# Moving one weight sum and the last adds of a Strassen-like MLP to GpSimd and ScalarE, and two sines to a later place

## The chip, the cores and the metric

The kernel runs on one core of one Trainium2 chip. The metric is the device time of one execution in microseconds (us), from its first to its last instruction with the small constant around them; lower is better.

## The reference, cut to what matters

Two transformer blocks run one after the other on x, 512 tokens by 1024 features, all in float32. The change lies in the MLP at the end of the first block, and at its border to the second block:

```python
# first_block, last two lines
h2 = rms_norm(x, norm_mlp_g[l])
x = x + jnp.square(jax.nn.relu(h2 @ w_up[l])) @ w_down[l]      # 1024 -> 4096 -> 1024
# second_block, first lines
cos_m, sin_m = rope_angles(positions, MLA_ROPE_DIM)            # sines and cosines of 28 angles a token
h = rms_norm_2(x, norm_gain[l])
proj = h @ w_in[l]
```

## The kernel before, in words

Every large product is made of three matmuls in a reduced float32 format: both operands are split into a high part (a rounded copy) and a low part (the rest), and high times high, high times low and low times high are summed in PSUM. ScalarE makes the high part of the weights (`split_hi`, `weight_hi`, tile `w_hi`), VectorE the low part by a subtraction (`split_lo`, `weight_lo`, tile `w_lo`); the same goes for the operands (`operand_hi`, `operand_lo`, tiles `op_hi` and `op_lo`). The order on each engine is written out by hand, and the engines are tied by counting semaphores.

The MLP is cut into 4 chunks of 1024 hidden features (`chunk(c)` on ScalarE and on VectorE, `mlp_up` and `mlp_down` on TensorE). In a chunk, TensorE first makes 8 tiles of the up projection, 24 matmuls of 512 columns each (L313), in the two banks of `proj` by turns; ScalarE takes each through a Relu and a Square into `acts` (L751, L753). Then comes the down projection of the chunk, in which the 2 by 2 blocks of `acts` and of the weights are combined by a scheme with 7 products in place of 8 (L1834). Three of the seven products are kept in PSUM over all four chunks (`RES`, six banks of `pa` and `pm`; the function `product` counts them in `res_made`) and are added to the residual stream `x_res` only at the end, by `drain` on VectorE (L1299 to L1309). The other four go through `proj` and are added to `x_res` in each chunk (tiles 8 to 15 of the chunk, `add`, L1321). TensorE waits with the next use of a bank of `proj` until the add before it has freed it (`tile_free`), and with each product until its weights and operands are there (`d_lo` counts the weights, `a_lo` the operands).

The combinations need sums of weight blocks. `t_two` is one of them; `w_sum[:, 0, 4:8]`, which is `t_two` less block `b21`, is another, of 128 x 2048 values. It shares its memory with a part of `w_lo` that the up projection reads until the chunk's eighth tile is done. `angles` (arguments of the sines) and `drained` share memory with `t_two`.

In the last chunk the third RMS norm and the first tiles of the second block follow without a pause: `norm_rstd(2, t)` on ScalarE, `token_scale(2, t)` on VectorE (L373), `token_turn(2, t)` on TensorE (8 transposes, L381), `token_hi` and `token_lo`. The last of the seven products is split for them: half of it (L1868, 12 matmuls), the transposes of token block 0, the other half, the transposes of block 1.

At the start of the MLP the first two tiles of the up projection are made in halves of 256 columns. The third tile needs the bank of the first, which ScalarE frees with its Relu.

Of the kernel before, what the change touches and what calls it, by code (L numbers as in the profile page):

```python
# [9 lines left out]
ALU = mybir.AluOpType  # L10
# [3 lines left out]
P = 128  # L14
# [68 lines left out]
def program(nc, x_in, wall, gains, head_par, sb_gains, b_if, *rest):  # L83
    *block2_in, out = rest
    with ExitStack() as ctx:
# [79 lines left out]
        b11, b21 = w_raw[:, 0], w_raw[:, 1]  # L165
        (a11, a12), (a21, a22) = [[acts[:, 4 * j:4 * j + 4, 2 * P * i:2 * P * (i + 1)] for j in range(2)] for i in range(2)]
# [90 lines left out]
        RES = (pa[:, 0:512], pa[:, 512:1024], pa[:, 1024:1536], pm[:, 0:512], pm[:, 512:1024], pm[:, 1024:1536])  # L257
# [218 lines left out]
        def _(pool):  # L476
# [52 lines left out]
            for r in (1, 2):  # L529
                if r == 2:  # L530
                    gp.wait_ge(S["t_made"], 4 * CHUNKS)
                gp.dma_start(row_gain[r][:, :], norm_rows[r - 1:r].broadcast_to([P, DM])).then_inc(S["rows_landed"], 16)
# [4 lines left out]
            gp.memset(causal[:, :], 0.0).then_inc(S["causal0"], 1)  # L537
            gp.wait_ge(S["causal0"], 1)
# [28 lines left out]
        def _(act):  # L567
# [165 lines left out]
            a.wait_ge(S["angles"], len(ANGLES))  # L733
            a.activation(sine[:, :, :], A3, ACT.Sin)
            a.activation(cosine[:, :, :], C3, ACT.Sin).then_inc(S["trig"], 1)
            a.preload_act_table_set("natural_log_exp_and_others")

# [6 lines left out]
            def chunk(c):  # L744
# [34 lines left out]
                operand_hi(0, a21)  # L779
                a.wait_ge(S["res_made"], 3 * c + 2)  # L780
# [11 lines left out]
            with a.Fori(0, CHUNKS) as c:  # L792
                chunk(c)

# [259 lines left out]
        def _(dve):  # L1054
# [236 lines left out]
            def drain(c, u):  # L1291
                x = [x_res[:, 2 * i + u, 512 * j:512 * (j + 1)] for i in range(2) for j in range(2)]
                z = drained[:, u]
                if u == 0:
                    v.wait_ge(S["res_made"], 3 * CHUNKS)
                    v.wait_ge(S["t_made"], 4 * CHUNKS)
                    v.wait_ge(S["d_lo"], 7 * c + 6)
                v.wait_ge(S["tile_free"], T_MLP + 16 * c + 9 + 4 * u)
# [9 lines left out]
                for i in (2, 3):  # L1308
                    v.tensor_tensor(x[i], x[i], z, ALU.add).then_inc(S["r_sum"], 1)  # L1309
                v.wait_ge(S["r_sum"], 7 * u + 7)  # L1310

            def chunk(c, first=False, last=False):
# [52 lines left out]
                if last:  # L1365
                    drain(c, 0)
# [803 lines left out]
```

## Time and profile before

| | |
|---|---|
| median of 3 runs | 1238.46 us (1238.39 to 1240.06) |
| the profiled execution, its own time | 1240.14 us |
| its span, first to last instruction | 1237.9 us |
| TensorE busy | 1217.6 us, 98% of the span |
| VectorE busy | 784.2 us, 63% |
| ScalarE busy | 637.1 us, 51% |
| GpSimd busy | 72.1 us, 6% |

A busy time is the share in which an instruction is in flight. TensorE's 20.3 us without one lie in few places, so these places, and not the shares, say what there is to be had. The profiled execution is 1.7 us above the median of the runs.

### The profile page before, as it was taken

What the parts mean: (1) busy time and instruction counts of PE and PEld (TensorE: products, weight loads), DVE (VectorE), ACT (ScalarE), POOL (GpSimd) and SP (SyncE); (2) the same over time, 40 slices, a digit from 0 to 9 for tenths busy, and PEclk for the clock granted to TensorE, in tenths of its full rate; (3) what the DMA queues carried; (4) which work ended last, traced back from release to release, by engine and by line L of the source; (5) the groups of instructions that cost most, each with busy time, mean ns of one, the idle gap of its engine ahead of it and who ended that gap; (6) DMA issues with size and microseconds to landing.
All of it is one profiled execution on the core that took longest, in us unless ns stands there. A gap on an engine that the chain in (4) does not pass through costs nothing.

```text
span 1237.9 us, 15568 instructions
## 1 busy us (share of the span) xinstructions
PE 1217.6 (98%) x5820; PEld 991.9 (80%) x5820; DVE 784.2 (63%) x1226; ACT 637.1 (51%) x926; POOL 72.1 (6%) x148
## 2 busy tenths in 40 slices
PE   8999999999999999999999999989999999999998
PEld 7888888888888888888888888868867777777887
DVE  7735544683564466469377483797579989656671
ACT  7635544563564462554444452545466555566820
POOL 2101110210111021000000000000000000000000
PEclk9999999999999999999999999999999999999999
DMA  5321322322132226214216123124213333535621
GB/s 212 123 95 39 110 68 76 102 88 95 37 111 68 77 102 224 102 34 148 91 40 216 50 102 136 34 85 162 77 68 111 113 135 111 218 123 179 238 69 68
DMA packets 25605, 134.21 MB, mean 108 GB/s; under 512 B 3336, under 2 KB 3512, under 8 KB 12752
## 3 DMA queue, kind: packets, MB, share of 16 engines
q1 hardware_dynamic: 16224, 107.14, 25.1%
q0 software_dynamic: 4720, 16.90, 3.9%
q10 hardware_dynamic: 4608, 9.44, 2.0%
q8 instruction: 35, 0.57, 0.2%
q14 instruction: 18, 0.15, 0.0%
HBM read 121.92 MB, written 11.55 MB: 108 GB/s over the span
## 4 chain that ended last, share of the span: by engine, by line
PE 87%; DVE 9%; issue 2%; ACT 1%; DMA 0%; ACTq 0%; DVEq 0%
PE proj L313 64%; PE proj L1834 5%; PE pm L1834 2%; PE pa L1834 2%; PE pm L1748 1%; PE pa L1759 1%; PE pa L2024 1%; DVE w_lo L286 1%; PE pa L1720 1%; PE pm L1730 1%; DVE idx L1468 1%; PE proj L1769 1%; PE pa L1769 1%; PE pa L2004 1%; PE pa L1739 1%
## 5 line engine op out<-in xcount | busy, mean ns | idle before, releaser
L313 PE MATMUL proj<-h_hi,w_hi 128*128 128x512 f32 (+1 forms) x848 | 332.5, 392 | 3.6 <-ACT acts L751 2.6
L313 PE MATMUL proj<-h_hi,w_lo 128*128 128x512 f32 (+1 forms) x848 | 327.7, 386 | 0.0
L313 PE MATMUL proj<-h_lo,w_hi 128*128 128x512 f32 (+1 forms) x848 | 327.3, 386 | 0.0
L286 DVE TENSOR_TENSOR w_lo<-w_raw,w_hi 128x2048 fp32r<-128x2048 f32 x84 | 191.5, 2288 | 58.7 <-ACT w_hi L280 58.4
L280 ACT ACTIVATE w_hi<-w_raw 128x2048 fp32r<-128x2048 f32 x84 | 159.6, 1913 | 67.3 <-PE proj L1834 46.9
L313 PEld LDWEIGHTS proj<-h_hi,w_hi 128*128 128x128 f32 x848 | 159.8, 188 | 39.8 <-issue 6.4
L313 PEld LDWEIGHTS proj<-h_hi,w_lo 128*128 128x128 f32 x848 | 159.6, 188 | 32.5
L313 PEld LDWEIGHTS proj<-h_lo,w_hi 128*128 128x128 f32 x848 | 159.8, 188 | 31.9 <-issue 1.0
L313 PE MATMUL proj<-w_hi,h_hi 128*128 128x512 f32 (+1 forms) x288 | 112.8, 392 | 0.3 <-issue 0.3
L313 PE MATMUL proj<-w_lo,h_hi 128*128 128x512 f32 (+1 forms) x288 | 111.6, 388 | 0.0
L313 PE MATMUL proj<-w_hi,h_lo 128*128 128x512 f32 (+1 forms) x288 | 111.4, 387 | 0.0
L751 ACT ACTIVATE acts<-proj 128x512 f32<-128x512 f32 x32 | 19.0, 594 | 97.8 <-PE proj L313 97.8
L313 PEld LDWEIGHTS proj<-w_hi,h_hi 128*128 128x128 f32 x288 | 54.1, 188 | 14.1 <-issue 3.5
L313 PEld LDWEIGHTS proj<-w_lo,h_hi 128*128 128x128 f32 x288 | 54.0, 188 | 10.9
L313 PEld LDWEIGHTS proj<-w_hi,h_lo 128*128 128x128 f32 x288 | 54.1, 188 | 10.4
L945 ACT ACTIVATE p_sb<-p_sb,mx 128x128 f32<-128x128 f32 (+1 forms) x64 | 35.2, 551 | 28.6 <-DVE mx L1557 28.6
L1834 PE MATMUL proj<-w_hi,op_hi 128*128 128x512 f32 x120 | 46.9, 391 | 2.5 <-DVE x_res L1321 2.5
L1834 PE MATMUL proj<-w_hi,op_lo 128*128 128x512 f32 x120 | 46.7, 389 | 0.0
L1834 PE MATMUL proj<-w_lo,op_hi 128*128 128x512 f32 x120 | 46.7, 389 | 0.0
L1329 DVE TENSOR_TENSOR w_sum<-b,b 128x2048 f32<-128x2048 f32 x4 | 9.2, 2292 | 56.8 <-PE proj L313 56.8
L1166 DVE SCALAR_TENSOR_TENSOR tok<-pm,floor 128x4 f32<-128x4 f32 x8 | 1.3, 162 | 67.9 <-ACT y_tok L659 67.9
L1321 DVE TENSOR_TENSOR x_res<-x_res,proj 128x512 f32<-128x512 f32 x40 | 26.7, 683 | 12.7 <-PE proj L1834 12.1
(455 smaller groups left out, 2083.7 us busy)
## 6 DMA issues: line engine op xcount, KB each, us to landing
w_raw<-in_wall SPq DMA_DIRECT2D x92, 1024.0 KB, 5.0
b<-in_wall SPq DMA_DIRECT2D x8, 1024.0 KB, 6.1
gates<-gate_st ACTq DMA_DIRECT2D x24, 256.0 KB, 2.0
m_all<-gates POOLq DMA_DIRECT2D x2, 1280.0 KB, 7.8
x_res<-in_x ACTq DMA_DIRECT2D x4, 512.0 KB, 5.1
bc<-gate_rows POOLq DMA_DIRECT2D x8, 256.0 KB, 3.4
x_res<-in_x POOLq DMA_DIRECT2D x4, 512.0 KB, 4.2
x<-x_res POOLq DMA_DIRECT2D x1, 2048.0 KB, 7.7
```

What stands on the lines that cost most here:

```text
L280: nc.scalar.activation(w_hi[:, slot, 4 * half:4 * half + 4, :], w_raw[:, half], ACT.Copy)\
L286: nc.vector.tensor_tensor(w_lo[:, slot, 4 * half:4 * half + 4, :], w_raw[:, half], w_hi[:, slot, 4 * half:4 * half + 4, :], ALU.subtract)\
L313: mm = nc.tensor.matmul(proj[:, bank, 0:cols] if tokens else proj[:, bank, toks], lhsT, rhs, start=(k == 0 and q == 0), stop=(k == kts - 1 ...
L751: a.activation(acts[:, i], proj[:, i % 2], ACT.Relu).then_inc(S["tile_free"], 1)
L945: a.activation(x, x, ACT.Exp, bias=mx[:, u, i:i + 1], accum_out=row_sum[:, u, i:i + 1])\
L1321: done = v.tensor_tensor(x, x, proj[:, i % 2], op)
L1468: v.scalar_tensor_tensor(idx[:, c], rel[h % 2][:, c], w_idx[:, i, h:h + 1], idx[:, c] if h else causal[:, 384 - P * i:512], ALU.mult, ALU. ...
L1720: mm = t_.matmul(pa[:, LOW[i]:LOW[i] + P * (i + 1)], a_[:, 0, P * i:P * (i + 1)], b_[:, 1, 0:P * (i + 1)], start=(x == 0), stop=(x == 2))
L1730: mm = t_.matmul(pm[:, TRI[i]:TRI[i] + SEQ - P * i], keys[r, P * i:P * (i + 1)], queries_[r, P * i:], start=True, stop=True)
L1739: mm = t_.transpose(pa[:, o:o + P], beta[:, LOW[i] + P * j:LOW[i] + P * (j + 1)], ident[:, :])
L1769: mm = t_.matmul(out_bank(t), y[:, k, c], w[:, 1, k, :], start=(k == 0 and q == 0), stop=(k == KT - 1 and q == 2))
L1834: mm = t_.matmul(banks[u], x[:, operand, k, P * u:P * (u + 1)], w[:, slot, 4 * half + k, :], start=(start and k == 0 and q == 0), stop=(st ...
```

## The change

Four edits, all in the MLP and at its end:

- The sum `w_sum[:, 0, 4:8]` is made by GpSimd in each of the 4 chunks, in place of VectorE. It starts when the first kept product of the chunk is made (`res_made`).
- The sines and cosines are computed by ScalarE behind the second Relu and Square of the first chunk, in place of ahead of the first weight copies of the chunk.
- The kept products are drained in another way: ScalarE copies the first two banks to `drained`, VectorE adds the other four, GpSimd adds the partial sums to `x_res`, in eight additions of 128 x 512. Two banks of `RES` change places for it.
- In the last chunk VectorE's order is another.

```diff
-        RES = (pa[:, 0:512], pa[:, 512:1024], pa[:, 1024:1536], pm[:, 0:512], pm[:, 512:1024], pm[:, 1024:1536])
+        RES = (pa[:, 0:512], pa[:, 512:1024], pa[:, 1024:1536], pm[:, 1024:1536], pm[:, 0:512], pm[:, 512:1024])
...
+            for c in range(CHUNKS):
+                gp.wait_ge(S["t_made"], 4 * c + 3)
+                gp.wait_ge(S["b21_landed"], 16 * c + 16)
+                gp.wait_ge(S["res_made"], 3 * c + 1)
+                gp.tensor_tensor(w_sum[:, 0, 4:8], t_two[:, :, :], b21, ALU.subtract).then_inc(S["t_made"], 1)
+            gp.wait_ge(S["d_lo"], 7 * CHUNKS - 4)
...
+            for u in range(2):
+                gp.wait_ge(S["r_sum"], u + 1)
+                gp.tensor_tensor(x_quarter[u][0][0], x_quarter[u][0][0], drained[:, u], ALU.add).then_inc(S["x_drained"], 1)
+            for u in range(2):
+                gp.wait_ge(S["r_sum"], u + 3)
+                gp.tensor_tensor(x_quarter[u][0][1], x_quarter[u][0][1], drained[:, u], ALU.add).then_inc(S["x_drained"], 1)
+            gp.wait_ge(S["tile_free"], T_END1 - 4)
+            for u in range(2):
+                gp.wait_ge(S["r_sum"], u + 5)
+                for j in range(2):
+                    gp.tensor_tensor(x_quarter[u][1][j], x_quarter[u][1][j], drained[:, u], ALU.add).then_inc(S["x_drained"], 1)
...
-            a.wait_ge(S["angles"], len(ANGLES))
-            a.activation(sine[:, :, :], A3, ACT.Sin)
-            a.activation(cosine[:, :, :], C3, ACT.Sin).then_inc(S["trig"], 1)
-            a.preload_act_table_set("natural_log_exp_and_others")
...
                 for i in range(4):
                     square(i)
+                    if first and i == 1:
+                        a.wait_ge(S["angles"], len(ANGLES))
+                        a.activation(sine[:, :, :], A3, ACT.Sin)
+                        a.activation(cosine[:, :, :], C3, ACT.Sin).then_inc(S["trig"], 1)
+                        a.preload_act_table_set("natural_log_exp_and_others")
...
+                if last:
+                    a.wait_ge(S["t_made"], 4 * c + 4)
+                    a.wait_ge(S["d_lo"], 7 * c + 3)
+                    for u in range(2):
+                        a.activation(drained[:, u], RES[u], ACT.Copy).then_inc(S["r_sum"], 1)
...
+            def drain_add(u, r, after):
+                v.wait_ge(S["x_drained"], after)
+                v.tensor_tensor(drained[:, u], drained[:, u], RES[r + u], ALU.add).then_inc(S["r_sum"], 1)
...
                 operand_lo(0, a21, c, 5)
-                v.tensor_tensor(w_sum[:, 0, 4:8], t_two[:, :, :], b21, ALU.subtract).then_inc(S["t_made"], 1)
                 weight_lo(1, 1, b12[:, :, :], c, 5)
```

What this makes of three places of the program. On GpSimd, between the load of the first norm's gains and the store of `x_res` to memory (`x`), there stood before:

```order
L532 DMA row_gain_84<-in_norm_rows 128x1024
L532 DMA row_gain_85<-in_norm_rows 128x1024 [waits t_made]
L535 DMA x<-x_res 128x4x1024 [waits tile_free]
```

and now:

```order
L530 DMA row_gain_84<-in_norm_rows 128x1024
L535 TENSOR_TENSOR w_sum<-t_two,w_raw 128x2048 [waits res_made,b21_landed,t_made] x4
L538 DMA row_gain_85<-in_norm_rows 128x1024 [waits t_made,d_lo]
L541 TENSOR_TENSOR x_res<-x_res,drained 128x512 [waits r_sum] x2
L544 TENSOR_TENSOR x_res<-x_res,drained 128x512 [waits r_sum] x2
L549 TENSOR_TENSOR x_res<-x_res,drained 128x512 [waits r_sum,tile_free]
L549 TENSOR_TENSOR x_res<-x_res,drained 128x512
L549 TENSOR_TENSOR x_res<-x_res,drained 128x512 [waits r_sum]
L549 TENSOR_TENSOR x_res<-x_res,drained 128x512
L552 DMA x<-x_res 128x4x1024 [waits tile_free]
```

GpSimd has 12 new instructions with two inputs from SBUF each; the load of the second gains stands behind four of them. On VectorE in the last chunk, around the first half of the drain (`b_82` is the block `b22`; `w_lo`, `op_lo` are the low parts of weights and operands, and `x_res<-x_res,proj` are the adds of tiles 8 and 9), the rows were:

```order
L1285 TENSOR_TENSOR w_lo<-b_82,w_hi 128x2048 [waits d_hi]
L1321 TENSOR_TENSOR x_res<-x_res,proj 128x512 [waits tile_made,tile_free]
L1299 TENSOR_TENSOR x_res<-x_res,pa 128x512 [waits d_lo,tile_free,t_made,res_made]
L1300 COPY drained<-pa 128x512
L1302 TENSOR_TENSOR drained<-drained,pm 128x512 [waits r_sum]
L1304 TENSOR_TENSOR x_res<-x_res,drained 128x512 [waits r_sum]
L1306 TENSOR_TENSOR drained<-drained,pa 128x512 [waits r_sum]
L1309 TENSOR_TENSOR x_res<-x_res,drained 128x512 [waits r_sum]
L1309 TENSOR_TENSOR x_res<-x_res,drained 128x512
L1321 TENSOR_TENSOR x_res<-x_res,proj 128x512 [waits tile_made,tile_free,r_sum]
```

and now:

```order
L1317 TENSOR_TENSOR drained<-drained,pm 128x512 [waits x_drained,res_made]
L1317 TENSOR_TENSOR drained<-drained,pm 128x512 [waits x_drained]
L1309 TENSOR_TENSOR w_lo<-b_82,w_hi 128x2048 [waits d_hi]
L1328 TENSOR_TENSOR x_res<-x_res,proj 128x512 [waits tile_made,tile_free,x_drained]
L1313 TENSOR_TENSOR op_lo<-acts,op_hi 128x1024 [waits a_hi]
L1328 TENSOR_TENSOR x_res<-x_res,proj 128x512 [waits tile_made,tile_free]
L1328 TENSOR_TENSOR x_res<-x_res,proj 128x512 [waits tile_made,tile_free,x_drained]
L1328 TENSOR_TENSOR x_res<-x_res,proj 128x512
L1317 TENSOR_TENSOR drained<-drained,pa 128x512 [waits x_drained]
L1317 TENSOR_TENSOR drained<-drained,pm 128x512 [waits x_drained]
```

Seven instructions between the adds of tiles 8 and 9 are gone, as are seven between tiles 12 and 13; four remain, and three of VectorE's steps now wait for GpSimd (`x_drained`). On ScalarE, where the MLP begins (behind the last `token_hi` of the second norm), there stood:

```order
L734 ACT_TABLE_LOAD
L734 ACTIVATE sine<-angles_100 128x112 [waits angles]
L735 ACTIVATE cosine<-angles_102 128x112
L736 ACT_TABLE_LOAD
L280 ACTIVATE w_hi<-w_raw 128x2048 [waits tile_made]
L280 ACTIVATE w_hi<-w_raw 128x2048 [waits tile_made,w_landed1]
L751 ACTIVATE acts<-proj 128x512 [waits tile_free,tile_made]
```

and now:

```order
L281 ACTIVATE w_hi<-w_raw 128x2048 [waits tile_made,w_landed0]
L281 ACTIVATE w_hi<-w_raw 128x2048 [waits tile_made,w_landed1]
L763 ACTIVATE acts<-proj 128x512 [waits tile_free,tile_made]
L765 ACTIVATE acts<-acts 128x512 [waits tile_free]
L763 ACTIVATE acts<-proj 128x512 [waits tile_made]
L765 ACTIVATE acts<-acts 128x512 [waits tile_free]
L773 ACT_TABLE_LOAD
L773 ACTIVATE sine<-angles_100 128x112 [waits angles]
L774 ACTIVATE cosine<-angles_102 128x112
L775 ACT_TABLE_LOAD
```

The two sines and their two table loads have moved behind the first two Relus.

## Rows read from the trace of the kernel before

**Rows 1.** The page: busy time, share of the span, instructions of each engine.

```profile
PE 1217.6 (98%) x5820; PEld 991.9 (80%) x5820; DVE 784.2 (63%) x1226; ACT 637.1 (51%) x926; POOL 72.1 (6%) x148
```

**Rows 2.** Stretches: length, busy time by engine (instructions), granted clock, DMA share, GB/s.

```profile
552.00:796.00 244.00, 244.00 (x1078) 202.03 (x1077) 157.47 (x108) 110.39 (x101) 0.00 (x0) 1.00 0.30 104
796.00:835.00 39.00, 36.20 (x157) 28.77 (x155) 37.02 (x34) 22.22 (x19) 0.53 (x1) 1.00 0.19 64
```

**Rows 3.** TensorE's waits from 490 to 860: total, times, longest.

```profile
PE pa L381 <- DVE xs L373: 3.6, 1, 3.6
PE proj L313 <- ACT acts L751: 2.6, 1, 2.6
PE proj L1834 <- DVE x_res L1321: 2.5, 1, 2.5
```

**Rows 4.** TensorE in order of time: start, length, instruction, idle before.

```profile
513.81 0.28 PE L313 MATMUL proj<-h_hi,w_lo 128*128 128x256 f32 x1
...
806.79 0.39 PE L1834 MATMUL pm<-w_hi,op_hi 128*128 128x512 f32 x1
...
823.07 0.50 PE L1834 MATMUL proj<-w_hi,op_hi 128*128 128x512 f32 x1 [2.49 <-DVE x_res L1321]
...
834.31 0.39 PE L1868 MATMUL proj<-w_lo,op_hi 128*128 128x512 f32 x1
838.34 1.70 PE L381 MATMUL pa<-ident,xs 128*128 128x128 f32 x8 [3.65 <-DVE xs L373]
839.69 0.78 PE L1868 MATMUL proj<-w_hi,op_hi 128*128 128x512 f32 x1
...
843.66 1.03 PE L381 MATMUL pm<-ident,xs 128*128 128x128 f32 x8
```

**Rows 5.** The chain that ended last: start, length, what, how many.

```profile
516.69 34.55 PE proj L313 x144
...
752.55 43.53 PE proj L313 x192
```

**Rows 6.** ScalarE in order of time, where the MLP begins.

```profile
506.54 1.28 ACT L734 ACT_TABLE_LOAD   x1
...
512.44 3.71 ACT L280 ACTIVATE w_hi<-w_raw 128x2048 fp32r<-128x2048 f32 x2
516.06 0.58 ACT L751 ACTIVATE acts<-proj 128x512 f32<-128x512 f32 x1
```

**Rows 7.** VectorE in order of time, in the last chunk.

```profile
801.13 1.23 DVE L1353 TENSOR_TENSOR acts<-acts,op_sum 128x1024 f32<-128x1024 f32 x1
802.27 2.28 DVE L1285 TENSOR_TENSOR w_lo<-t_two,w_hi 128x2048 fp32r<-128x2048 f32 x1
804.47 1.22 DVE L1289 TENSOR_TENSOR op_lo<-op_sum,op_hi 128x1024 fp32r<-128x1024 f32 x1
...
817.50 0.69 DVE L1299 TENSOR_TENSOR x_res<-x_res,pa 128x512 f32<-128x512 f32 x1
...
837.01 1.28 DVE L373 SCALAR_TENSOR_TENSOR xs<-x_res,rstd,row_gain 128x1024 f32<-128x1024 f32 x1
```

**Rows 8.** GpSimd in order of time: two selects.

```profile
50.72 0.29 POOL L510 TENSOR_SCALAR_AFFINE_SELECT keep<-keep 128x128 f32<-128x128 f32 x1
...
127.76 2.37 POOL L515 TENSOR_SCALAR_AFFINE_SELECT decay<-decay 128x128 f32<-128x128 f32 x1
```

**Rows 9.** GpSimd's groups by shape: busy us, mean ns.

```profile
L539 POOL TENSOR_SCALAR_AFFINE_SELECT causal<-causal 128x128 f32<-128x128 f32 x1 | 0.3, 287 | 0.1
...
L488 POOL CAST wg_lo<-wg_zero 128x704 fp32r<-128x704 f32 x1 | 0.8, 778 | 0.0
```

**Rows 10.** VectorE, one subtraction in order of time.

```profile
127.68 2.29 DVE L286 TENSOR_TENSOR w_lo<-w_raw,w_hi 128x2048 fp32r<-128x2048 f32 x1 [0.24 <-ACT w_hi L280]
```

**Rows 11.** VectorE's lines of one tile: ns min/median/max, first and last start.

```profile
L1138 DVE TENSOR_TENSOR silu<-silu,conv x8: 784/789/790, 50.8 to 440.6; 128x512 f32<-128x512 f32 x8
...
L1185 DVE TENSOR_TENSOR silu<-silu,gate_a x8: 691/693/695, 80.9 to 463.3; 128x512 f32<-128x512 f32 x8
```

More of the change, by code:

```diff
@@ L165, in program @@
         b11, b21 = w_raw[:, 0], w_raw[:, 1]
+        x_quarter = [[[x_res[:, 2 * i + u, 512 * j:512 * (j + 1)] for j in range(2)] for i in range(2)] for u in range(2)]
         (a11, a12), (a21, a22) = [[acts[:, 4 * j:4 * j + 4, 2 * P * i:2 * P * (i + 1)] for j in range(2)] for i in range(2)]
@@ L536, in _ @@
             gp.wait_ge(S["norm_turned"], KT + 2 * TB)
-            gp.memset(causal[:, :], 0.0).then_inc(S["causal0"], 1)
-            gp.wait_ge(S["causal0"], 1)
+            gp.memset(causal[:, :], 0.0).then_inc(S["c0"], 1)
+            gp.wait_ge(S["c0"], 3)
             gp.affine_select(out=causal[:, 384:512], in_=causal[:, 384:512], compare_op=ALU.is_ge, fill=NEG,
@@ L742, in operand_hi, with chunk @@
                 a.activation(op_hi[:, slot], src, ACT.Copy).then_inc(S["a_hi"], 1)
-            def chunk(c):
+            def chunk(c, first=False, last=False):
                 g = G_MLP + 2 * c
@@ L790, in chunk @@
                 split_hi(g + 2, 1, 1, used=n + 12)
-            with a.Fori(0, CHUNKS) as c:
+            chunk(0, first=True)
+            with a.Fori(1, CHUNKS - 1) as c:
                 chunk(c)
+            chunk(CHUNKS - 1, last=True)
             a.preload_act_table_set("natural_log_exp_and_others")
@@ L1359, in chunk @@
                 operand_lo(0, a21, c, 5)
-                v.tensor_tensor(w_sum[:, 0, 4:8], t_two[:, :, :], b21, ALU.subtract).then_inc(S["t_made"], 1)
                 weight_lo(1, 1, b12[:, :, :], c, 5)
                 operand_lo(1, a12, c, 6)
+                if last:
+                    v.wait_ge(S["res_made"], 3 * c + 3)
+                    for u in range(2):
+                        drain_add(u, 4, u + 1)
                 weight_lo(0, 0, b22[:, :, :], c, 6)
+                if last:
+                    v.wait_ge(S["x_drained"], 2)
                 add(8, 0, j=0)
+                operand_lo(2, a22, c, 7)
+                add(9, 1, j=0)
                 if last:
-                    drain(c, 0)
-                add(9, 1, j=0)
-                operand_lo(2, a22, c, 7)
+                    v.wait_ge(S["x_drained"], 4)
                 add(10, 0, 2, j=1)
+                if last:
+                    for u in range(2):
+                        drain_add(u, 2, u + 3)
+                    add(11, 1, 3, j=1)
                 v.wait_ge(S["t_made"], 4 * c + 4)
                 weight_lo(0, 1, w_sum[:, 0, 4:8], c, 7)
-                add(11, 1, 3, j=1)
-                split_lo(g + 2, 1, 0)
+                if not last:
+                    add(11, 1, 3, j=1)
+                    split_lo(g + 2, 1, 0)
                 add(12, 0, j=1)
-                if last:
-                    drain(c, 1)
-                else:
+                if not last:
                     split_lo(g + 2, 1, 1)
@@ L1380, in chunk @@
                 if last:
+                    split_lo(g + 2, 1, 0)
                     token_scale(2, 0)
                     split_lo(g + 2, 1, 1)
+                    v.wait_ge(S["x_drained"], 8)
                 add(14, 2, j=0, op=ALU.subtract)
```

27 lines of the change are left out of this document (3 added, 24 removed).

## The prediction

> **What bounds the kernel now.** I read the page's totals first: TensorE has a matmul in flight for 1217.6 of 1237.9 us [rows 1]. Only its 20.3 us of idle time, and slow stretches, can be won, and anything that makes it wait is lost in full. Next the table of stretches: from 552 to 796, three of the four chunks, TensorE is busy for all of the 244 us, VectorE for 157 [rows 2]. Nothing can be won there; a new wait can only cost. In 796 to 835, the down projection of the last chunk, VectorE is busy for 37.0 of 39 us and TensorE misses 2.8 [rows 2]: here VectorE is the bound. The list of TensorE's waits then names the three places that the edits touch: 2.6 us for a Relu of ScalarE at the start of the MLP, 2.5 us for an add and 3.6 us for a norm scaling of VectorE at its end [rows 3].
>
> **The sines.** TensorE stops at 513.9 and goes on at 516.69, when ScalarE has freed the first bank [rows 3, 4, 5]. ScalarE reached this Relu at 516.06, behind two weight copies of 3.71 us together, which began at 512.44 though the norm's last copy ended at 506.5 [rows 6]. Without table loads and sines ahead of them the copies end near 510.3, and the Relu only has to wait for its tile, which the chip makes before 513.9. The 2.8 us go. The 144 matmuls behind the wait took 34.55 us, where 192 at full rate took 43.53 [rows 5], which is 32.65 for 144: another 1.9 us went to a stretch at the lower of the two clock levels, which I take to follow the idle time. So this edit is worth -4.7 us. In their new place the sines and two table loads take about 3.2 us (they end at 512.44 at the latest, and 2 x 1.28 of it is loads [rows 6]) between the second and the third Relu, 5.4 us apart (24 matmuls of 0.227 us, from 43.53/192 [rows 5]): hidden.
>
> **The weight sum on GpSimd.** VectorE loses a subtraction of 2.2 us a chunk, behind which, in chunks 0 to 2, nobody waits. What GpSimd's version costs is seen in no row; it has two inputs in SBUF and 2048 columns. Its cast of 704 columns took 0.78 us with one input [rows 9]: 2048 columns are 2.25 us for one pass, 4.5 us if the two inputs are read one after the other. These are the bounds of its length T. I take 4.5, since the rows below show the two engines to take turns at reading. By the Trainium skill ("GPSIMD Engine Reference", Performance versus the Vector engine) such a subtraction of 2048 takes 4497 ns; the sum would be the same.
>
> The question is what it does to VectorE. A select of GpSimd takes 0.29 us alone [rows 9]. One that began at 127.76, just behind a VectorE subtraction with two SBUF inputs (127.68, 2.29 us [rows 10]), took 2.37 us [rows 8] and ended 0.15 us after it: it was shut out for the whole instruction. The other way round, the product of 512 columns that VectorE begins at 50.76 in each head, 0.04 us behind a select of 0.29 us (50.72 [rows 8]), takes 0.79 us, the same shape elsewhere 0.69 [rows 11]: it waits until the select's short read is over. GpSimd also gets its turn between VectorE instructions that stand back to back. So I expect that VectorE's instructions with two SBUF inputs wait for GpSimd's whole T. The Trainium skill says so too ("SBUF — State Buffer", Who interferes with whom: the shared pair is an exclusive lock, and the second to issue fully blocks); this trace agrees, for short instructions.
>
> Where it falls: GpSimd may start when the first kept product is done, 5.44 us (24 x 0.227) into the down projection; in the last chunk, whose third product begins at 806.79 [rows 4], that is 5.44 us earlier, 801.35. VectorE is in a combination of `acts` until 802.3, then come the low part of `t_two` (802.27) and of operand 2 (804.47, done at 805.6) [rows 7]. TensorE wants both for the third kept product at 806.79 [rows 4]. The slack is 1.2 us. If GpSimd takes its turn at 802.3, the third product starts T - 1.2 late: 3.3 us with T = 4.5, 1.05 with 2.25. This is the same in each chunk. For chunks 0 to 2: +9.9 us (+3.1 at the lower bound). ScalarE's copies behind it are not held up, and the load that waits for the sum (`t_made`) now starts within 2 us of its old time, with 5 us to spare.
>
> **The last chunk and the norm.** I carry the chain through with the durations of rows 7: 2.2 us a weight part, 1.14 an operand part, 0.6 to 0.7 an add of 512, 1.2 the norm scaling; a GpSimd add of 512 columns is a quarter of T, 1.2 us. The drain of 817.50 and its twin (seven instructions, some 5 us each) no longer stand ahead of the adds for which TensorE waited at 823.07 and ahead of the scaling at 837.01 [rows 4, 7].
>
> If GpSimd did not disturb VectorE: the 2.5 us wait goes, small waits of 0.6 us go, the fifth to seventh products run without a gap until 831.3, the scaling of block 0 is ready at 832.7 in place of 838.3, and everything behind is 5.6 us earlier. The 1.8 us of lower clock behind the wait of 3.65 us go too (transposes 838.34 to 839.69 in place of 0.79 us, half product 839.69 to 843.66 in place of 2.72 [rows 4]). Together -7.4 us.
>
> If it does: the third product ends at 815.5, the fourth at 821.0. VectorE has the low parts at 809.1 and 810.2, then takes turns with GpSimd's first two adds (1.2 us each), has the last operand before the drain at 819.3, two drain adds at 820.7, waits for GpSimd's third add until 821.1, makes the low part of `b22` until 823.3 and frees tile 8 at 823.9. TensorE waited for it since 821.0: +3.0 us. The seventh product's first half ends at 837.6. The scaling of block 0 waits for GpSimd's adds of the second half, which alternate with two weight parts of VectorE, and is done at 841.1, where it was 838.3. So +2.9 us for the last chunk as a whole, with its gains and losses; its old lower clock stays.
>
> **The clock.** Of the three waits of 2.5 to 3.65 us, two had a stretch at the lower level behind them, at 1.9 and 1.8 us. In the locked case there are five new waits of 3.0 to 3.3 us. I take two of them to cost 1.8 us each: +3.6; the bounds are none and five (0 and +9).
>
> **The sum**, against the profiled execution's own 1240.14 us: -4.7 +9.9 +2.9 +3.6 = +11.7, 1251.8; against the median of the runs, which is 1.7 lower, about 1250.2 us.
>
> **The rivals.**
> - No lock that matters: GpSimd's long read is served in between, or it gets its turn only once VectorE pauses (one late turn, after the part of operand 2, would hold up nothing, since the weight part after it ends at 804.47 + 1.14 + 2.2 = 807.8 and is wanted at 806.79 + 5.44 = 812.2). For it: all seen cases are reads of 128 to 256 columns. Against it: a select was shut out for 2.3 us, and got its turn at once when the subtraction ended. Then -4.7 - 7.4 = -12.1: 1226.4 us.
> - A short T. It decides the sign: the loss of the first three chunks is 3(T - 1.2), and below T of about 3 us it no longer eats the gains. At 2.25: -4.7 +3.1 -3.2 -1.8 = -6.6: 1231.9 us.
> - The end of the MLP gives back what it wins, through waits of three engines for each other (`r_sum`, `x_drained`), and GpSimd costs nothing else: the sines alone remain, -4.7: 1233.8 us.
> - The wait at 513.9 stays, because the halves of 256 columns cause the lower clock and not the idle time: this would add 1.9 us to each of the cases.
>
> **Chances.** Locked for a T of 3.5 us or more, 0.61: 1243 (T of 4, no lower clock) to 1256 (T of 4.5, all five). No lock that matters 0.25; short T 0.07; sines alone 0.07. The first is the forecast, its own range 1243 to 1256. Within 0.2% (2.5 us, about what a measurement of this kernel tells from no change) falls only a T near 3 us: 0.03, out of the first and third. The range that leaves out no more than 2 in 10 reaches down into the case without a lock: 1226 to 1256.
>
> **What the profile of the changed kernel would show.** GpSimd's four subtractions: length 5 us or more, of which the first 0.9 is the wait; VectorE's low part of `t_two` at 6.5 us in place of 2.29; TensorE idle for 3.3 us ahead of the third kept product in all four chunks, released by VectorE's operand part; a chunk 85 us long in place of 81.6. Without a lock VectorE's row stays at 2.29 and the chunk at 81.6. TensorE without an idle time near 514 and no matmul of 0.43 us there would show the sines' part right. The scaling of block 0 tells the end of the chunk. Most likely to make me wrong is how GpSimd reads two inputs of 2048 columns: no row shows it.

## The result, and the profile after

The changed kernel takes 1252.14 us (median of 6 runs, 1249.11 to 1253.78), the kernel before 1239.18 us (6 runs, 1238.39 to 1240.06): a ratio of 1.0102, 95% interval 1.0093 to 1.0112. The forecast was 1250.2 us, slower. The profiled execution took 1250.44 us, with a span of 1248.7.

The page of the changed kernel, its totals (the answer to [rows 1]):

```profile
PE 1217.8 (98%) x5820; PEld 991.0 (79%) x5820; DVE 791.4 (63%) x1212; ACT 638.3 (51%) x928; POOL 111.2 (9%) x160
```

TensorE has the same work in the same 1217.8 us. All that was lost is idle time. The table of stretches says where, with columns as in [rows 2]:

```profile
552.00:796.00 244.00, 234.22 (x1018) 192.66 (x1017) 157.31 (x101) 104.78 (x95) 15.46 (x3) 0.99 0.29 101
796.00:835.00 39.00, 33.26 (x146) 26.93 (x145) 31.24 (x18) 19.56 (x17) 15.00 (x6) 1.00 0.16 57
634.00:719.00 85.00, 81.77 (x355) 67.27 (x354) 54.70 (x35) 36.41 (x33) 5.16 (x1) 0.98 0.28 99
```

In 552 to 796 TensorE now misses 9.8 of 244 us, where it missed none. From one third kept product to the next (560.77, 647.45 and 733.98 below and in the table) a chunk lasts 86.7 and 86.5 us, where it lasted 81.6; in 634 to 719, a length of 85, TensorE works for 81.8. TensorE's waits (the answer to [rows 3]):

```profile
PE pm L1851 <- DVE op_lo L1313: 13.1, 4, 3.3
PE pa L382 <- DVE xs L374: 3.5, 1, 3.5
PE proj L1851 <- DVE x_res L1328: 2.4, 1, 2.4
```

Four waits of 3.3 us for VectorE's low part of an operand are new. The wait of 2.6 us for a Relu is gone. The wait for the scaling is about as long as it was, and so is the one for an add of VectorE, but that is now the add of tile 8 and no longer that of tile 9. The reason for the four, in the last chunk, GpSimd first:

```profile
810.63 5.16 POOL L535 TENSOR_TENSOR w_sum<-t_two,w_raw 128x2048 f32<-128x2048 f32 x1 [79.99 <-PE pa L1851]
...
829.86 3.33 POOL L544 TENSOR_TENSOR x_res<-x_res,drained 128x512 f32<-128x512 f32 x1
```

Then VectorE (the answer to [rows 7]):

```profile
810.07 1.23 DVE L1360 TENSOR_TENSOR acts<-acts,op_sum 128x1024 f32<-128x1024 f32 x1
811.22 6.72 DVE L1309 TENSOR_TENSOR w_lo<-t_two,w_hi 128x2048 fp32r<-128x2048 f32 x1
817.86 1.21 DVE L1313 TENSOR_TENSOR op_lo<-op_sum,op_hi 128x1024 fp32r<-128x1024 f32 x1
818.99 3.37 DVE L1309 TENSOR_TENSOR w_lo<-w_raw,w_hi 128x2048 fp32r<-128x2048 f32 x1
822.28 2.31 DVE L1313 TENSOR_TENSOR op_lo<-acts,op_hi 128x1024 fp32r<-128x1024 f32 x1
...
831.98 0.68 DVE L1328 TENSOR_TENSOR x_res<-x_res,proj 128x512 f32<-128x512 f32 x1
832.57 1.70 DVE L1313 TENSOR_TENSOR op_lo<-acts,op_hi 128x1024 fp32r<-128x1024 f32 x1
...
847.83 2.28 DVE L374 SCALAR_TENSOR_TENSOR xs<-x_res,rstd,row_gain 128x1024 f32<-128x1024 f32 x1
```

GpSimd starts at 810.63, waits until VectorE's combination ends at 811.30, and is done at 815.79: 4.49 us of its own. VectorE's low part of `t_two`, 2.28 us long before, lasts from 811.22 to 817.94: its own 2.2 us begin when GpSimd has ended. Where VectorE has one input in PSUM, GpSimd's reading costs it nothing: the add of a tile of `proj` at 831.98 takes its usual 0.68 us inside GpSimd's add (829.86 to 833.19). The operand part behind it, both inputs in SBUF, waits for GpSimd's end and takes 1.70 in place of 1.22. Even the norm scaling (847.83) is held up. TensorE in order of time (the answer to [rows 4]):

```profile
560.77 0.47 PE L1851 MATMUL pm<-w_hi,op_hi 128*128 128x512 f32 x1 [3.32 <-DVE op_lo L1313]
...
562.26 0.63 PE L1851 MATMUL pm<-w_lo,op_hi 128*128 128x512 f32 x1
...
815.51 0.39 PE L1851 MATMUL pm<-w_lo,op_hi 128*128 128x512 f32 x1
819.21 0.47 PE L1851 MATMUL pm<-w_hi,op_hi 128*128 128x512 f32 x1 [3.32 <-DVE op_lo L1313]
...
832.80 0.47 PE L1851 MATMUL proj<-w_hi,op_hi 128*128 128x512 f32 x1 [2.42 <-DVE x_res L1328]
...
850.16 0.33 PE L382 MATMUL pa<-ident,xs 128*128 128x128 f32 x1 [3.50 <-DVE xs L374]
```

A matmul of 0.39 us is one at the full rate, of 0.63 one at the lower of the two clock levels; they start 0.23 and 0.43 us apart. Both kernels run the same 5820 matmuls in the same order, so that the start of one can be set against the start of the same one. The column on the right is the sum of all gains and losses up to there:

| matmul, by its number in the trace | before | after | after less before |
|---|---|---|---|
| 2484, behind the Relu | 516.69 | 513.74 | -2.95 |
| 2496, behind the lower clock of before | 521.05 | 516.49 | -4.56 |
| 2676, third kept product, chunk 0 | 561.96 | 560.77 | -1.19 |
| 2688, behind a lower clock | 564.68 | 565.18 | +0.50 |
| 3036, third kept product, chunk 1 | 643.59 | 647.45 | +3.86 |
| 3043, behind a lower clock | 645.17 | 650.53 | +5.36 |
| 3396, third kept product, chunk 2 | 725.19 | 733.98 | +8.79 |
| 3410, behind that wait | 728.36 | 737.31 | +8.94 |
| 3756, third kept product, chunk 3 | 806.79 | 819.21 | +12.43 |
| 3816, behind the add of tile 9 | 823.07 | 835.62 | +12.55 |
| 3864, transposes of block 0 | 838.34 | 850.16 | +11.82 |
| 3877, in the last half product | 841.97 | 852.25 | +10.28 |
| 3972, second block | 860.10 | 870.93 | +10.82 |

ScalarE where the MLP begins (the answer to [rows 6]):

```profile
506.22 3.71 ACT L281 ACTIVATE w_hi<-w_raw 128x2048 fp32r<-128x2048 f32 x2
511.06 0.60 ACT L763 ACTIVATE acts<-proj 128x512 f32<-128x512 f32 x1 [1.13 <-PE proj L314]
...
515.22 1.28 ACT L773 ACT_TABLE_LOAD   x1
```

The copies begin 6.2 us earlier, and the Relu waits for its tile, not for ScalarE.

### The profile page after: what moved, and what is told of

Same layout as the page of the kernel before. It is cut to its first block, busy times and chain, and to the rows that moved or that the text cites. A ratio compares the mean times of both kernels' runs of the same rounds, so it can differ in the third digit from the quotient of the medians.

```text
span 1248.7 us, 15534 instructions
## 1 busy us (share of the span) xinstructions
PE 1217.8 (98%) x5820; PEld 991.0 (79%) x5820; DVE 791.4 (63%) x1212; ACT 638.3 (51%) x928; POOL 111.2 (9%) x160
## 4 chain that ended last, share of the span: by engine, by line
PE 88%; DVE 8%; issue 2%; ACT 1%; DMA 0%; ACTq 0%; DVEq 0%
PE proj L314 64%; PE proj L1851 6%; PE pm L1851 2%; PE pa L1851 2%; DVE w_lo L287 2%; PE pm L1765 1%; PE pa L1776 1%; PE pa L2041 1%; PE pa L1737 1%; PE pm L1747 1%; DVE idx L1485 1%; PE proj L1786 1%; PE pa L1786 1%; DVE op_lo L1313 1%; PE pa L2021 1%
## 5 line engine op out<-in xcount | busy, mean ns | idle before, releaser
L535 POOL TENSOR_TENSOR w_sum<-t_two,w_raw 128x2048 f32<-128x2048 f32 x4 | 20.6, 5156 | 324.2 <-PE pa L1851 324.2
```

The costliest lines, as they stand in the source:

```text
L535: gp.tensor_tensor(w_sum[:, 0, 4:8], t_two[:, :, :], b21, ALU.subtract).then_inc(S["t_made"], 1)
```

## The experiments

Each time stands beside runs of the kernel before on the same chip (1239.3 to 1239.9 us); the ratio is to these. Of each trace I show what decides. "Interval" is the 95% one.

### The weight sum back on VectorE

```diff
-            for c in range(CHUNKS):
-                ...
-                gp.tensor_tensor(w_sum[:, 0, 4:8], t_two[:, :, :], b21, ALU.subtract).then_inc(S["t_made"], 1)
...
                 operand_lo(0, a21, c, 5)
+                v.tensor_tensor(w_sum[:, 0, 4:8], t_two[:, :, :], b21, ALU.subtract).then_inc(S["t_made"], 1)
```

> The changed kernel with one thing undone: the weight sum of every chunk is made by VectorE again, behind operand_lo(0, a21). The sines' new place, the new drain and VectorE's other order stay. Theory (GpSimd's long subtraction shuts VectorE out; this, and not the drain, is the loss): the three waits of 3.3 us in chunks 0 to 2 go and the two stretches at the lower clock behind them, 5.06 + 4.86 + 3.55 = 13.5 us by the shift of TensorE's matmuls between the two traces. In the last chunk ScalarE's copies to drained now wait for VectorE's sum and stand ahead of the high part of b12, so that TensorE waits about 5.3 us for tile 8 in place of 3.3 and 2.7 us: that chunk stays within 1 us of the changed kernel's. About 1237 us, VectorE's low part of t_two at 2.28 us, chunks 81.6 us apart. Rival (the drain with GpSimd is what costs, through waits of three engines for each other): no less than 1245 us.

1240.02 us, ratio 1.0001 (interval 0.9991 to 1.0010). The waits:

```profile
PE proj L1847 <- DVE x_res L1323: 5.2, 1, 5.2
PE pa L382 <- DVE xs L374: 3.5, 1, 3.5
```

The four waits are gone; 12.1 us come back, so that GpSimd's sum is the loss. The absolute time was expected 3 us lower. The wait for tile 8 came as expected (5.2), but 10 matmuls ran at the lower clock behind it (2.1 us), and from chunk 2 to the second block this kernel loses 5.1 us against the one before (-4.5 to +0.6 by the matmuls), the changed one 1.9 (+8.9 to +10.8): 3.2 more, not within the 1 us allowed.

### The sines alone, and the sum alone

The kernel before with ScalarE's edit alone:

```diff
-            a.activation(sine[:, :, :], A3, ACT.Sin)
...
+                    if first and i == 1:
+                        ...
+                        a.activation(sine[:, :, :], A3, ACT.Sin)
```

> The kernel before with the sines' move alone. Theory: -4.7 us as forecast (the traces of the two kernels show -4.4 us by TensorE's shift there): about 1234.7 us against 1239.2; no idle time near 514, ScalarE's third Relu waits for its tile. Rival (what is won at the start of the MLP is given back at its end, where VectorE is the bound and its work hangs on loads and not on TensorE): within 1 us of the kernel before.

1235.34 us, ratio 0.9967 (0.9954 to 0.9979), 4.5 us less. TensorE's matmuls are 4.64 us earlier at the first kept products and 4.66 us earlier at the transposes of block 0: nothing is given back. And the kernel before with GpSimd's sum alone:

```diff
+                    for c in range(CHUNKS):
+                        ...
+                        gp.wait_ge(S["res_made"], 3 * c + 1)
+                        gp.tensor_tensor(w_sum[:, 0, 4:8], t_two[:, :, :], b21, ALU.subtract).then_inc(S["t_made"], 1)
...
-                v.tensor_tensor(w_sum[:, 0, 4:8], t_two[:, :, :], b21, ALU.subtract).then_inc(S["t_made"], 1)
```

> The kernel before with the weight sum on GpSimd alone, started behind the first kept product of each chunk as in the change; sines and drain as before. Theory: 3.4 us in each of chunks 0 to 2, 2.3 us in the last one (VectorE has 2.28 us less to do there, so that the wait of 2.5 us shrinks to 1.5), which is 12.5 us, and up to two or three stretches at the lower clock of 1.5 to 1.7 us each: 1252 to 1256 us against 1239.2. Rival (the loss comes only with the sines' move or the new drain): 1243 us or less.

1259.37 us, ratio 1.0163 (1.0146 to 1.0180), above the range. The waits are those expected:

```profile
PE pm L1840 <- DVE op_lo L1295: 13.1, 4, 3.3
PE pa L381 <- DVE xs L373: 2.8, 1, 2.8
PE proj L313 <- ACT acts L757: 2.6, 1, 2.6
PE proj L1840 <- DVE x_res L1327: 2.4, 1, 2.4
```

What was mis-sized is the lower clock. It followed the waits of chunks 0, 1 and 3 and that for tile 9, for 13, 7, 13 and 9 matmuls: 42 x 0.20 = 8.4 us where at most 5 had been allowed. The wait for tile 9 did not shrink to 1.5. This trace also lacks the two lower-clock stretches of the kernel before, behind the Relu wait and behind the scaling (by the shift of the matmuls -1.6 us each), though both waits are there: whether a stretch follows a wait is not settled by the wait alone.

### The sum in pieces, and half of it

```diff
-                gp.tensor_tensor(w_sum[:, 0, 4:8], t_two[:, :, :], b21, ALU.subtract).then_inc(S["t_made"], 1)
+                for k in range(4):
+                    piece = gp.tensor_tensor(w_sum[:, 0, 4 + k], t_two[:, k], b21[:, k], ALU.subtract)
+                piece.then_inc(S["t_made"], 1)
```

> The changed kernel with GpSimd's weight sum in four instructions of 512 columns in place of one of 2048, at the same place; the work and the bytes are the same. GpSimd's adds of 512 columns took 1.3 us in the changed kernel. Theory (an instruction of one engine with two SBUF inputs holds out that of the other until it has ended, and the engines take turns between instructions): VectorE's part of t_two waits for one piece and takes about 3.4 us in place of 6.7, the operand part behind it waits for the next one and takes 2.3, so that TensorE waits for 2 x 1.15 less the slack of 1.2, about 1.2 us in place of 3.3, in each of the four chunks: 2.1 us less in each, and less or nothing of the 3.2 us at the lower clock: 1240.5 to 1244 us. Rival (the two engines share the memory's rate, so that the same bytes in the same stretch cost the same): the wait stays at 3.3 us and the time at 1250 to 1252.

1248.07 us, ratio 1.0065 (1.0048 to 1.0082). VectorE in chunk 0:

```profile
552.94 3.39 DVE L1311 TENSOR_TENSOR w_lo<-t_two,w_hi 128x2048 fp32r<-128x2048 f32 x1
556.25 2.30 DVE L1315 TENSOR_TENSOR op_lo<-op_sum,op_hi 128x1024 fp32r<-128x1024 f32 x1
558.48 3.38 DVE L1311 TENSOR_TENSOR w_lo<-w_raw,w_hi 128x2048 fp32r<-128x2048 f32 x1
```

And TensorE's waits:

```profile
PE proj L1853 <- DVE x_res L1330: 6.5, 4, 5.0
PE pm L1853 <- DVE op_lo L1315: 4.2, 4, 1.1
```

The same bytes at the same place cost 1.1 us a chunk in place of 3.3, with exactly the lengths that turn-taking gives (3.4 and 2.3). A shared rate is out. The time was missed: the pieces went on to hold up VectorE four times over (3.39, 2.30, 3.38 and 2.31 us), so that TensorE waited 0.5 us for the add of tile 8 in each of chunks 0 to 2, and in the last one the high part of b12 stood behind the late sum, with 5.0 us of wait for tile 8.

```diff
-                gp.tensor_tensor(w_sum[:, 0, 4:8], t_two[:, :, :], b21, ALU.subtract).then_inc(S["t_made"], 1)
+                gp.tensor_tensor(w_sum[:, 0, 4:6], t_two[:, 0:2], b21[:, 0:2], ALU.subtract).then_inc(S["c0"], 1)
...
                 operand_lo(0, a21, c, 5)
+                v.wait_ge(S["c0"], c + 3)
+                v.tensor_tensor(w_sum[:, 0, 6:8], t_two[:, 2:4], b21[:, 2:4], ALU.subtract).then_inc(S["t_made"], 1)
```

> The changed kernel with GpSimd's weight sum at its place, but of half the columns (1024); VectorE makes the other half behind operand_lo(0, a21), in 1.2 us. Theory (what TensorE waits is GpSimd's length less a slack of 1.2 us): GpSimd needs 2.3 us in place of 4.5, VectorE's part of t_two takes 4.5 us in place of 6.7, and TensorE waits about 1.1 to 1.3 us ahead of the third kept product in place of 3.3. In the last chunk ScalarE's copies wait for VectorE's half with b12 behind them, as in the first experiment (1240.0 us). 1240.0 + 3 x 1.2 = 1243.6, up to 1246 with the lower clock. Rival (a fixed price of a switch between the engines, not the length): 3 us a chunk remain, 1248 us or more.

1244.79 us, ratio 1.0038 (1.0023 to 1.0052), inside the range. VectorE, then TensorE's waits:

```profile
552.88 4.51 DVE L1309 TENSOR_TENSOR w_lo<-t_two,w_hi 128x2048 fp32r<-128x2048 f32 x1
```

```profile
PE pm L1853 <- DVE op_lo L1313: 4.3, 4, 1.1
```

GpSimd's half took 2.94 us, 0.65 of it the wait for VectorE's combination. The wait follows the length: 3.3 us for 4.5, 1.1 for 2.3, none without it. So each us of GpSimd's read beyond the slack of 1.2 is a us of TensorE's. In the last chunk the wait for tile 8 was 5.0 us, as in the first experiment.

### The sum on GpSimd, but later

Four kernels, each the changed one with the sum of chunks 0 to 2 at a place where VectorE should have room. First behind the low part of `b22`:

```diff
                 gp.wait_ge(S["res_made"], 3 * c + 1)
+                if c < CHUNKS - 1:
+                    gp.wait_ge(S["d_lo"], 7 * c + 6)
```

> The changed kernel, with GpSimd's weight sum of chunks 0 to 2 started later: behind VectorE's sixth low part of weights (b22), in place of behind the first kept product. It is as long and reads the same; the last chunk is untouched. Theory (the loss is the lock, at a place where VectorE has only 1.2 us of slack): at the new place VectorE's add of tile 8 reads PSUM and its part of operand a22 has over 3 us of slack, so that the 3.3 us waits in chunks 0 to 2 go and nothing or up to 0.5 us a chunk comes in their place (the add of tile 11 stands behind the low part of w_sum). 1250.4 - 13.5 = about 1237 us, up to 1239. Which VectorE instruction is long moves: the part of t_two is 2.28 us again, that of operand a22 about 5 us in place of 1.2. Rival (a sum on GpSimd costs its 3.4 us a chunk wherever it stands, for instance through the load that waits for it, which starts 10 us later): 1248 us or more.

1250.41 us, ratio 1.0091 (1.0073 to 1.0109): the rival's number, not mine. VectorE in chunk 0:

```profile
567.77 5.33 DVE L1315 TENSOR_TENSOR op_lo<-acts,op_hi 128x1024 fp32r<-128x1024 f32 x1
573.02 1.99 DVE L1330 TENSOR_TENSOR x_res<-x_res,proj 128x512 f32<-128x512 f32 x3
```

The operand part is the long one, as expected, and it had the room. What I had not followed is the queue: the add of tile 9 stands behind it, at 573.02, and TensorE wanted its bank at 571.0. Waits of 2.6 us took the place of those of 3.3 in three chunks (the fourth in this row is that for tile 8 in the last chunk):

```profile
PE proj L1853 <- DVE x_res L1330: 10.3, 4, 2.6
```

So the place matters, but this run doesn't show that it could be free.

Next behind the adds of tiles 8 and 9, with the add of tile 11 ahead of the low part of `w_sum`:

```diff
+                if c < CHUNKS - 1:
+                    gp.wait_ge(S["tile_free"], T_MLP + 16 * c + 10)
...
+                if not last:
+                    add(11, 1, 3, j=1)
                 v.wait_ge(S["t_made"], 4 * c + 4)
                 weight_lo(0, 1, w_sum[:, 0, 4:8], c, 7)
                 if not last:
-                    add(11, 1, 3, j=1)
```

> GpSimd's weight sum of chunks 0 to 2 later still than in the run before: behind VectorE's adds of tiles 8 and 9, for the second of which TensorE waited there, and with the add of tile 11 ahead of the low part of w_sum; the last chunk as in the change. What VectorE then has in GpSimd's 4.6 us reads PSUM (the adds of tiles 10 and 11), but for nothing else. Theory (only VectorE's instructions with two SBUF inputs are held out, and only what TensorE wants behind them costs): no wait of TensorE over 0.5 us in chunks 0 to 2, VectorE's adds at 0.68 us while GpSimd's subtraction runs, the chunks 81.6 us apart, and 1236.5 to 1239 us, the changed kernel less 13.5. Rival (GpSimd's sum costs 3 us a chunk wherever it stands; its late end delays the load that waits for it): a wait moves to the start of the next chunk, 1245 us or more.

1248.31 us, ratio 1.0070 (1.0054 to 1.0087): missed again, by the same kind of step. VectorE, chunk 0:

```profile
576.37 2.29 DVE L1311 TENSOR_TENSOR w_lo<-w_sum,w_hi 128x2048 fp32r<-128x2048 f32 x1 [1.18 <-ACT w_hi L753]
578.58 2.29 DVE L287 TENSOR_TENSOR w_lo<-w_raw,w_hi 128x2048 fp32r<-128x2048 f32 x1
580.78 0.68 DVE L1330 TENSOR_TENSOR x_res<-x_res,proj 128x512 f32<-128x512 f32 x1
```

GpSimd's sum now runs beside adds that read PSUM, undisturbed, but the low part of `w_sum` is later, and the add of tile 12 stands behind it and behind a part that nobody wants yet. TensorE waited until 581.61, for 2.4 us. Next, moved ahead of that part:

```diff
                 weight_lo(0, 1, w_sum[:, 0, 4:8], c, 7)
-                if not last:
-                    split_lo(g + 2, 1, 0)
                 add(12, 0, j=1)
                 if not last:
+                    split_lo(g + 2, 1, 0)
                     split_lo(g + 2, 1, 1)
```

> As the run with the weight sum behind the add of tile 9, and in every chunk VectorE's add of tile 12 also ahead of the first low part of the next chunk's weights. There the late sum pushed the low part of w_sum back, the next low part and the add of tile 12 stood behind it, and TensorE waited 2.4 us a chunk for that add. Theory (GpSimd's sum has no price of its own, only what stands behind it on VectorE and is wanted): the add of tile 12 comes at 578.7 in place of 580.8, TensorE wants it at 579.1, and no wait over 0.5 us is left in chunks 0 to 2. The next chunk's loads, which wait for the sum, land about when ScalarE wants them. Chunks 81.6 to 82.5 us apart, 1237 to 1240 us. Rival (a late sum on GpSimd is paid somewhere in any case, next through the loads and ScalarE's high parts): 2 us or more a chunk remain, 1244 to 1248 us.

1249.19 us, ratio 1.0074 (1.0058 to 1.0091): missed a third time, and above the rival's range too. The add of tile 12 came at 578.64, as expected; but I had put both low parts of the next chunk's weights (579.23, 4.52 us) ahead of the add of tile 13, which TensorE wanted at 582.3; it went on at 584.4. The last step puts it between the two:

```diff
                 add(12, 0, j=1)
                 if not last:
                     split_lo(g + 2, 1, 0)
-                    split_lo(g + 2, 1, 1)
                 add(13, 1, j=1)
+                if not last:
+                    split_lo(g + 2, 1, 1)
```

> As the run before it with the late sum, with one add moved: that of tile 13 stands between the two low parts of the next chunk's weights in chunks 0 to 2, in place of behind both, where TensorE waited for it for 2.0 us (VectorE had it at 583.7 to 584.3, it was wanted at 582.1). Theory (GpSimd's 4.6 us have no price of their own): the add ends near 582.1, no wait over 0.5 us is left in chunks 0 to 2, chunks are 81.6 to 82.2 us apart, and the time is 1237 to 1240 us. Rival (a late sum is paid somewhere in any case): 2 us or more a chunk remain, at the start of the next chunk's up projection or as a stretch at the lower clock, 1243 to 1248 us.

1239.69 us, ratio 1.0007 (0.9997 to 1.0016), inside the range and 12.4 us less than the changed kernel. The long read and the adds inside it, GpSimd and then VectorE:

```profile
569.76 4.61 POOL L537 TENSOR_TENSOR w_sum<-t_two,w_raw 128x2048 f32<-128x2048 f32 x1 [98.73 <-DVE x_res L1330]
```

```profile
571.24 1.29 DVE L1330 TENSOR_TENSOR x_res<-x_res,proj 128x512 f32<-128x512 f32 x2 [1.66 <-PE proj L1854]
573.96 1.29 DVE L1330 TENSOR_TENSOR x_res<-x_res,proj 128x512 f32<-128x512 f32 x2 [1.43 <-PE proj L1854]
```

The subtraction on GpSimd is as long as in the change (4.61 us), and TensorE misses 0.3 of 244 us:

```profile
552.00:796.00 244.00, 243.68 (x1070) 199.90 (x1069) 148.86 (x104) 108.64 (x101) 13.85 (x3) 1.00 0.29 104
```

The rival, 2 us or more a chunk, is out. What a sum on GpSimd costs in these runs is of two kinds: what waits behind the instruction that it holds out (the change and the first placement), and what waits behind the low part of `w_sum`, which a late sum delays (the second and third, where none of VectorE's instructions shown was held out). Some 0.6 us a chunk remain by the shift of the matmuls (-4.6 to -2.8 us over three chunks). The adds stand in another order here too; no run has that order with the sum on VectorE, so the 0.6 us belong to both together.

### The drain

With the sum on VectorE, ScalarE's copies behind the high parts of b12 and its operand, GpSimd's adds kept (VectorE's first sum into `drained` also waits for both copies):

```diff
-                if last:
-                    ...
-                        a.activation(drained[:, u], RES[u], ACT.Copy).then_inc(S["r_sum"], 1)
                 a.wait_ge(S["res_made"], 3 * c + 2)
                 weight_hi(1, 1, b12[:, :, :])
...
                 operand_hi(1, a12)
+                if last:
+                    ...
+                        a.activation(drained[:, u], RES[u], ACT.Copy).then_inc(S["r_sum"], 1)
```

> The changed kernel with the weight sum back on VectorE, as in the first experiment, and ScalarE's two copies to drained moved behind the high parts of b12 and its operand. There TensorE waited for 5.6 us for tile 8, since these copies waited for VectorE's sum with the high part of b12 behind them. GpSimd's eight adds to x_res stay. Theory: VectorE's part of b12 starts on time; GpSimd's adds of 1.3 us each hold out VectorE's parts three times before the add of tile 8, and TensorE waits there for about 3.3 us in place of 5.6. About 1237 us in place of 1240. Against the run without GpSimd, made beside it, the difference is what its eight adds cost or bring. Rival (the adds on GpSimd bring more than they hold up): as fast as the run without GpSimd or faster.

1237.67 us, ratio 0.9984 (0.9974 to 0.9993). The waits:

```profile
PE pa L382 <- DVE xs L374: 3.5, 1, 3.5
PE proj L1848 <- DVE x_res L1323: 3.3, 1, 3.3
```

As expected, 3.3 in place of 5.2. And without GpSimd, the drain in the order of need (`drain_first` makes what token block 0 or 1 lacks, `drain_rest` what 2 or 3 lack):

```diff
                 add(9, 1, j=0)
                 if last:
...
+                    drain_first(0, n + 10)
...
                 add(10, 0, 2, j=1)
...
                 add(12, 0, j=1)
...
+                if last:
+                    drain_first(1, n + 12)
+                    token_scale(2, 0)
...
                 add(13, 1, j=1)
...
                 add(14, 2, j=0, op=ALU.subtract)
                 if last:
...
                     token_lo(2, 0)
+                    drain_rest(0)
...
                 add(15, 3, j=0, op=ALU.subtract)
+                if last:
+                    drain_rest(1)
...
```

> No GpSimd at all: the sines' new place, the weight sum on VectorE, ScalarE's two copies to drained behind the high parts of b12 and its operand, and the 12 remaining steps of the drain on VectorE in the order in which the token blocks are wanted: three for block 0 behind the add of tile 9, three for block 1 behind that of tile 12, ahead of the scaling of block 0, and the six of blocks 2 and 3 only behind the first low part of the norm. Expected: the wait of 2.5 us for the add of tile 9 goes, that of 3.65 us for the scaling of block 0 shrinks to under 1; but VectorE has no pause from there to the scaling of block 3, and has only two copies of 0.69 us less to do, so that at most 2 to 3 us of this are left when TensorE wants blocks 2 and 3. With the sines' 4.5: 1231.5 to 1234.5 us against 1239.5. Rival (the order doesn't matter, VectorE's total at the end does): 1235, that of the sines alone.

1230.99 us, ratio 0.9931 (0.9914 to 0.9948): faster than both kernels, just below the expected range. The waits:

```profile
PE proj L314 <- DVE h_lo L391: 1.6, 1, 1.6
PE pm L382 <- DVE xs L374: 1.4, 2, 1.2
PE pa L382 <- DVE xs L374: 0.9, 1, 0.9
PE proj L1854 <- DVE x_res L1331: 0.2, 1, 0.2
```

The scaling of block 0 came 6.5 us earlier than with the sines alone; of this 2.6 us were left in the second block, since VectorE has no pause up to the scaling of block 3. Between the run with GpSimd's adds kept and this one lie 6.7 us by the medians, but only 2.8 us by the matmuls of the two traces at the second block. Eight of the former's ten runs took about 1237.7 us at a mean granted clock of 0.996; its trace is of one that took 1235.16 at 0.999. So over half of the 6.7 us looks like matmuls at the lower clock in executions of which there is no trace. GpSimd's eight adds and the order made for them cost the rest; how much of that is the lock and how much the order isn't told apart. Last, this kernel with the late sum of chunks 0 to 2 and the order of the adds that went with it:

```diff
+            for c in range(CHUNKS - 1):
+                ...
+                gp.wait_ge(S["tile_free"], T_MLP + 16 * c + 10)
+                gp.tensor_tensor(w_sum[:, 0, 4:8], t_two[:, :, :], b21, ALU.subtract).then_inc(S["t_made"], 1)
...
+                if last:
+                    v.tensor_tensor(w_sum[:, 0, 4:8], t_two[:, :, :], b21, ALU.subtract).then_inc(S["t_made"], 1)
```

> The run without GpSimd and with the drain in the order of need (1231.0 us, all weight sums on VectorE), with the weight sums of chunks 0 to 2 on GpSimd, late, and the adds in the order of the run beside this one; the last chunk keeps its sum on VectorE. Theory: free or nearly so, 1231 to 1233 us; nothing is gained either, since VectorE has pauses in these chunks. Rival: 5 us or more slower than 1231.

1232.80 us, ratio 0.9951 (0.9934 to 0.9968): 1.8 us over the run above, three times the 0.6 us of a late sum. Inside the range, free it is not quite, and it brings nothing.

## Why the prediction was right, step by step

- **The sines**, -4.7 us forecast: -4.56 by the matmuls, -4.5 as a run of their own. The stretch at the lower clock left with the idle time, and the sum-alone trace has the half tiles of 256 columns and the wait but no such stretch, so the rival that the half tiles cause it is out.
- **The length T**, 4.5 us taken between 2.25 and 4.5: 4.49 behind the wait, 4.58 to 4.61 where GpSimd started freely. The value was right, but the reason given for it from rows doesn't carry: that the two engines take turns says nothing of how GpSimd reads its own two inputs. So 4.5 was the choice of the upper of two bounds, and no row spoke for it. (One pass by the cast is 0.78 us x 2048/704 = 2.27 us and not 2.25, which changes nothing.) By the Trainium skill ("GPSIMD Engine Reference", Performance versus the Vector engine) an add of 2048 float32 values takes 4497 ns (the table has the add, not the subtraction); the trace agrees.
- **The lock**, +3.3 us a chunk: 3.37, 3.36, 3.43 and 3.49 in the table, with `w_lo` at 6.72 us where 6.5 was forecast. The runs with pieces and with half the length bear out both the turns and T - 1.2. By the Trainium skill ("SBUF — State Buffer", Who interferes with whom) the engine that comes second is blocked for the whole instruction; the trace agrees.
- **The last chunk**, +2.9 as a whole: from +8.94 (chunk 2, behind its wait) to +11.82 at the transposes of block 0, which is 2.9. The wait for tile 9 went and one for tile 8 came, as forecast; that one was put at 3.0 us and was 2.42, and GpSimd's adds took 1.3 us and not 1.2.
- **The lower clock**, +3.6 for two stretches of 1.8: two came, of 1.69 and 1.50 us. One thing was wrong: "its old lower clock stays". Behind the scaling of block 0 the changed kernel's profiled execution has none, which gives 1.5 us back. The number of two was a guess between none and five, and that it came out is luck.
- **The sum**: +11.7 forecast for the profiled execution, +10.3 measured. The terms of the table: -4.56 +10.16 (three chunks' waits) +0.15 +3.19 (clock) +2.88 -1.54 +0.54 = +10.82 at the second block. The spans lie 10.8 us apart too; the time outside the span is 0.5 us shorter in the changed kernel (1.7 in place of 2.2). The missing stretch at the lower clock is the largest term that the forecast had otherwise.

The medians lie 13.0 us apart, and not 10.3. Three of the changed kernel's six runs took 1253.6 to 1253.8 us at a mean granted clock of 0.990 to 0.994, three 1249.1 to 1250.7 at 0.997 to 0.998. The number of waits with a lower clock behind them seems to differ between executions; only the profiled one has a trace, so for the others the mean clock is all there is to go by. The stated range of 1226 to 1256 us held the case without a lock as well; what the result bears out is the first case's own 1243 to 1256. The rivals fell by their own signs: no lock (VectorE's row would be 2.29 us and was 6.72), a short T (4.49 us measured), and an end that gives back the sines (the sines alone keep 4.7 us to the second block).

## What to carry to other kernels

An instruction moved to an idle GpSimd is not free when it reads two matrices from SBUF: in these traces it added its length to the VectorE instruction with such inputs that came next (2.28 us became 6.72), so lay it beside VectorE work that reads PSUM. Pieces help only in part: four of them still cost TensorE 1.1 us a chunk at a slack of 1.2, since each holds out another VectorE instruction. Follow the queue behind the instruction that is held out down to the first result somebody wants: three of my four placements failed one or two rows behind the instruction that was held out or late. When an engine is the bound only for a short end, sort its work by who needs it first: that order, together with two copies given to ScalarE, gained 4 us beyond the sines (1235.34 to 1230.99), while no weight sum on GpSimd gained anything. No run has the order without the copies.

## What the hardware showed that I had not expected

- While GpSimd read SBUF with two inputs, VectorE's adds with one input in PSUM ran at their usual 0.68 us, also two in a row (571.24, 1.29 us for both), and the norm scaling, with two inputs from SBUF, took 2.28 us in place of 1.28.
- GpSimd is held out in the same way: its adds of 128 x 512 took 1.3 us alone and 3.3 us behind a VectorE part of 2.2 us.
- The same wait doesn't always bring the lower clock: of the four waits of 3.3 us, two did in the changed kernel's trace and three with the sum alone, and the stretch that follows lasted between 6 and 13 matmuls of 0.43 us.
